# Hand-over from routing to experts: rows from slots by transposes, held gate loads, a shorter first row load

## What is computed

```
def hier_moe(h, w_group, b_group, w_expert, b_expert, w_gate, w_up, w_down):
    xf = xt.astype(F32)
    g_logits = xf @ w_group + b_group
    g_prob = jax.nn.softmax(g_logits, axis=-1)
    g_idx = jnp.argmax(g_logits, axis=-1)
    e_logits = (xf @ w_expert + b_expert).reshape(-1, N_GROUPS, EXP_PER_GROUP)
    e_sel = jnp.take_along_axis(e_logits, g_idx[:, None, None], axis=1)[:, 0]
    top_v, top_i = lax.top_k(jax.nn.softmax(e_sel, axis=-1), TOP_K)
    ...
    for e in range(N_EXPERTS):
        he = jax.nn.silu(xt @ w_gate[e]) * (xt @ w_up[e])
        y = y + combine[:, e:e + 1] * (he @ w_down[e]).astype(F32)

xp = gated_merge(xp, ...)                       # x += mixing part (through w_out)
xp = xp + hier_moe(rmsnorm(xp, g_ffn[l]), ...)  # x += experts
```

## Time and profile before

| | us |
|---|---|
| median of 3 runs | 1005.37 |
| lowest, highest | 1004.75, 1006.37 |
| profiled execution, its own time | 1005.73 |
| its span, first to last instruction | 1003.9 |
| the rest of its time, around the span | 1.8 |

### The profile page before, as it was taken

The page is one execution under the profiler, slowest core; times in us unless marked ns, Lnnn a source line. Parts: engine busy times, 40 slices in busy tenths (PEclk is TensorE's granted clock), DMA queues, the critical chain, the costliest instruction groups (busy, mean ns, idle before and its releaser), DMA issues.

```text
span 1003.9 us, 12085 instructions
## 1 busy us (share of the span) xinstructions
PE 986.0 (98%) x4614; PEld 810.5 (81%) x4614; DVE 674.6 (67%) x983; ACT 522.4 (52%) x700; POOL 150.5 (15%) x184
## 2 busy tenths in 40 slices
PE   9999999999999999999999999999999999999995
PEld 6888888888887887877877888789788888888884
DVE  6486875346656653443448457686889889888883
ACT  6744322345545553332452304544588687887783
POOL 1010001121120311121130000012012112121111
PEclk9999999999999999999999999999999999999999
DMA  9476567874361655973284345137899999999994
GB/s 348 144 221 145 134 142 234 252 224 159 135 232 61 244 195 188 348 283 140 95 314 164 105 173 224 55 128 286 345 401 403 380 404 391 392 405 380 403 404 93
DMA packets 125987, 245.27 MB, mean 244 GB/s; under 512 B 69072, under 2 KB 69376, under 8 KB 113600
## 3 DMA queue, kind: packets, MB, share of 16 engines
q1 hardware_dynamic: 105520, 172.51, 47.2%
q0 software_dynamic: 20112, 71.37, 21.6%
q10 hardware_dynamic: 288, 0.52, 0.2%
HBM read 203.07 MB, written 52.08 MB: 254 GB/s over the span
## 4 chain that ended last, share of the span: by engine, by line
PE 67%; issue 26%; DVE 3%; POOL 3%; ACT 1%; DMA 0%; POOLq 0%; SPq 0%; ACTq 0%; DVEq 0%
PE ps L481 16%; PE ps L483 16%; PE ps L482 16%; PE ps L1874 3%; PE ps L1875 3%; PE ps L1847 2%; PE ps L1909 2%; POOL x_exp L858 1%; POOL out_y L869 1%; PE ps L2017 1%; PE ps L2033 1%; PE ps L1968 1%; DVE w_lo L453 1%; PE ps L1891 1%; PE ps L2024 1%
## 5 line engine op out<-in xcount | busy, mean ns | idle before, releaser
L481 PE MATMUL ps<-w_hi,s_hi 128*128 128x512 f32 x640 | 255.6, 399 | 0.8 <-issue 0.8
L483 PE MATMUL ps<-w_lo,s_hi 128*128 128x512 f32 x640 | 249.7, 390 | 0.0
L482 PE MATMUL ps<-w_hi,s_lo 128*128 128x512 f32 x640 | 249.3, 390 | 0.0
L481 PEld LDWEIGHTS ps<-w_hi,s_hi 128*128 128x128 f32 x640 | 120.3, 188 | 26.4 <-issue 2.2
L482 PEld LDWEIGHTS ps<-w_hi,s_lo 128*128 128x128 f32 x640 | 120.3, 188 | 25.3 <-issue 1.0
L483 PEld LDWEIGHTS ps<-w_lo,s_hi 128*128 128x128 f32 x640 | 120.1, 188 | 25.4
L417 DVE TENSOR_TENSOR w_lo<-raw,w_hi 128x2048 fp32r<-128x2048 f32 x40 | 91.6, 2290 | 47.4 <-ACT w_hi L412 47.2
L1016 ACT ACTIVATE stage<-ps,x_rstd 128x512 f32<-128x512 f32 x64 | 44.0, 688 | 140.4 <-PE ps L483 140.0
L412 ACT CAST w_hi<-raw 128x2048 fp32r<-128x2048 f32 x40 | 76.2, 1910 | 16.8 <-DMA raw<-in_w_in 11.2
L453 DVE TENSOR_TENSOR lo_x<-raw_x,hi_x 128x2048 fp32r<-128x2048 f32 x32 | 72.5, 2286 | 6.9 <-ACT hi_x L430 6.9
L453 DVE TENSOR_TENSOR lo_x<-raw_x,w_hi 128x2048 fp32r<-128x2048 f32 x32 | 72.6, 2287 | 5.3 <-ACT w_hi L430 5.2
(11 more groups left out here) (308 smaller groups left out, 1830.7 us busy)
## 6 DMA issues: line engine op xcount, KB each, us to landing
raw<-in_w_in SPq DMA_DIRECT2D x30, 1024.0 KB, 8.5
raw_x<-in_w_gate SPq DMA_DIRECT2D x30, 1024.0 KB, 24.3
raw_x<-in_w_down SPq DMA_DIRECT2D x18, 1024.0 KB, 23.7
raw_x<-in_w_up SPq DMA_DIRECT2D x16, 1024.0 KB, 21.2
raw<-in_w_up SPq DMA_DIRECT2D x16, 1024.0 KB, 22.3
raw<-in_w_down SPq DMA_DIRECT2D x14, 1024.0 KB, 23.2
x_slots<-in_c_empty SPq DMA_DIRECT2D x4, 2112.0 KB, 21.1
x_exp<-x_slots POOLq DMA_DIRECT2D x16, 528.0 KB, 13.6
```

The lines of the kernel that those rows point to most:

```text
L481: nc.tensor.matmul(out, s_h, w_h, start=first, stop=False)
L482: nc.tensor.matmul(out, s_l, w_h, start=False, stop=False)
L483: return nc.tensor.matmul(out, s_h, w_l, start=False, stop=last)
```

## The change

There are six parts, all in the hand-over:

1. `BY_PRODUCT` goes from 3 to 2: `rows_a` is loaded after the dispatches of three tiles, not two, and only the last two tiles are placed by a one-hot product. DVE makes two one-hot matrices.
2. `slot_rows` uses transposes in place of float32 matmuls with the identity, and stands first in its PSUM banks.
3. PE's order changes, and two groups of transposes of the identity into otherwise unused banks are added (`keep_busy`, 12 and 6).
4. DVE scales the last tile's rows after `choose` and not ahead of it, in two halves: the first ahead of `place_first`, the second behind it (with a new semaphore `last_row`, for which PE waits).
5. ACT takes a root of a constant into a spare word right after the exponentials of the fourth tile, so that the table load for Sqrt stands there.
6. SP issues m = 6 and m = 7 only when all ten dispatches have landed, and `x_exp[0]` is loaded with its notes alone (128 rows x 32 floats).

```diff
--- before.py
+++ after.py
@@ -59,7 +59,7 @@
 LAM_INIT = 0.8 - 0.6 * math.exp(0.0)
 SINK = ROWS
 FILL_AT = 26
-BY_PRODUCT = 3
+BY_PRODUCT = 2
 FIRST_PARTS = ((0, 1), (1, 2), (2, 4), (4, 6), (6, 8))
 
 
@@ -156,7 +156,8 @@
     end[0] = GSUB + 4 * (DV + 2 * DK)
     r_bias = after("r_bias", [P, NG + NE], f32)
     gffn_col = after("gffn_col", [P, KC], f32)
-    lam = after("lam", [P, 4], f32)
+    lam_spare = after("lam", [P, 8], f32)
+    lam, spare = lam_spare[:, 0:4], lam_spare[:, 4:5]
     eps = after("eps", [P, 1], f32)
     x2_rms = after("x2_rms", [P, 2, TT], f32)
     x_rstd = after("x_rstd", [P, TT], f32)
@@ -344,7 +345,7 @@
     sel_ready, pos_ready, npass_ready = sem("sel_ready"), sem("pos_ready"), sem("npass_ready")
     row_ready, dispatched, meta_ready = sem("row_ready"), sem("dispatched"), sem("meta_ready")
     x_loaded = [sem("x_loaded0"), sem("x_loaded1")]
-    slots_ready, onehot_ready = sem("slots_ready"), sem("onehot_ready")
+    slots_ready, onehot_ready, last_row = sem("slots_ready"), sem("onehot_ready"), sem("last_row")
     sample_kept, rows_a_in = sem("sample_kept"), sem("rows_a_in")
     x_tr, xhi_ready, xlo_ready = sem("x_tr"), sem("xhi_ready"), sem("xlo_ready")
     silu_ready, act_ready = sem("silu_ready"), sem("act_ready")
@@ -612,6 +613,8 @@
                     sp.wait_ge(blocks_used, LAST - 2)
                 elif m < SPL:
                     sp.wait_ge(blocks_used, LAST - 1 + m - WR)
+                    if m >= SPL - 2:
+                        sp.wait_ge(dispatched, 16 * 2 * TT)
                 elif m == SPL:
                     sp.wait_ge(y_init, 16 * TT)
                     sp.wait_ge(sample_kept, 16)
@@ -854,7 +857,9 @@
 
         def load_rows(j, i):
 
-            if j == 0:
+            if j == 0 and i == 0:
+                dma(x_exp[0][:, D_MODEL:XW], x_slots[CAP * EXPERT[0]:CAP * EXPERT[0] + P, D_MODEL:XW]).then_inc(x_loaded[0], 16)
+            elif j == 0:
                 dma(x_exp[i % 2][:, :], x_slots[CAP * EXPERT[i]:CAP * EXPERT[i] + P, :]).then_inc(x_loaded[i % 2], 16)
             else:
                 pool.indirect_dma_start(out=x_exp[i % 2][:, :], out_offset=None, in_=x_slots,
@@ -1201,6 +1206,7 @@
                 source_hi(4, t, (0,))
             if n:
                 exps(ORDER[n - 1])
+        own(nc.scalar.activation(spare, eps[:, :], ACT.Sqrt))
         source_hi(4, ORDER[PT], (1,))
         square_x2(ORDER[PT])
         root_x2(ORDER[PT])
@@ -1633,10 +1639,10 @@
                     source_lo(2, PT)
 
 
-        def rows_of_tile(t):
+        def rows_of_tile(t, c0=0, c1=D_MODEL):
             rows = slice(0, P if t < PT else SAMPLE)
-            v.scalar_tensor_tensor(rows_out[rows, t, 0:D_MODEL], x2[rows, t, :], x2_rms[rows, 1, t:t + 1],
-                                   gffn[rows, :], ALU.mult, ALU.mult)
+            return v.scalar_tensor_tensor(rows_out[rows, t, c0:c1], x2[rows, t, c0:c1], x2_rms[rows, 1, t:t + 1],
+                                          gffn[rows, c0:c1], ALU.mult, ALU.mult)
 
         def root_of_tile(t):
             rows = slice(0, P if t < PT else SAMPLE)
@@ -1727,9 +1733,10 @@
         source_lo(4, ORDER[PT], (1,))
         place_rows(ORDER[PT - 1])
         root_of_tile(ORDER[PT])
-        rows_of_tile(ORDER[PT])
         choose(ORDER[PT])
+        rows_of_tile(ORDER[PT], 0, COLS)
         place_first(ORDER[PT])
+        rows_of_tile(ORDER[PT], COLS).then_inc(last_row, 1)
         place_rows(ORDER[PT])
 
         def count_slots():
@@ -2116,29 +2123,37 @@
         def placed_rows(n, half):
             t = ORDER[TT - BY_PRODUCT + n]
             pe.wait_ge(onehot_ready, n + 1)
+            if n == BY_PRODUCT - 1 and half:
+                pe.wait_ge(last_row, 1)
             for k in range(4):
                 last = mm(ps[:, half, k * P:(k + 1) * P], rows_out[:, t, rows_of(half, k)], onehot[:, n, :],
-                          start=n == 0 and k == 0, stop=n == BY_PRODUCT - 1 and k == 3)
+                          start=False, stop=n == BY_PRODUCT - 1 and k == 3)
             return last
 
         def slot_rows(half):
             pe.wait_ge(rows_a_in, 16)
             for k in range(4):
-                mm(ps[:, half, k * P:(k + 1) * P], rows_a[:, rows_of(half, k)], ident, start=False, stop=False)
+                mm(ps[:, half, k * P:(k + 1) * P], rows_a[:, rows_of(half, k)], ident, start=k == 0, stop=False,
+                   is_transpose=True)
+
+        def keep_busy(bank, count):
+            for _ in range(count):
+                transpose(ps[:, bank, 0:P], ident, ident)
 
         positions(PT - 1)
         logits(ORDER[PT], (0,))
         pe.wait_ge(p_evacuated, x2_done(ORDER[PT]))
         source(4, ORDER[PT], x2[:, ORDER[PT], :], (1,))
-        placed_rows(0, 0)
+        keep_busy(1, 12)
         logits(ORDER[PT], (1,))
-        placed_rows(0, 1)
-        for half in range(2):
-            placed_rows(1, half)
-        positions(PT)
         for half in range(2):
             slot_rows(half)
-            placed_rows(2, half).then_inc(x_tr, 1)
+            placed_rows(0, half)
+        positions(PT)
+        pe.wait_ge(x2_squared, TT)
+        keep_busy(3, 6)
+        for half in range(2):
+            placed_rows(1, half).then_inc(x_tr, 1)
         pe.wait_ge(row_ready, TT)
         for s in range(TT):
             last = mm(ps[:, 7, TT * NE:(TT + 1) * NE], ones16[:, :], sel[:, s, :], start=s == 0, stop=s == TT - 1)
```

## The result

The changed kernel took 1008.35 us in the median of 20 runs (1005.85 to 1011.85). The kernel before took 1006.31 beside it, also of 20 (1004.75 to 1009.69). The ratio is 1.0018, with a 95% interval of 1.001 to 1.0027: slower by 0.2%, or 1.8 us, where I forecast 1.2 us faster. The median lies above my range, and 4.15 us above the 1004.2 that I forecast. Of these, 0.94 us is the kernel before, whose three runs shown ahead had a median of 1005.37; the other 3.2 is the forecast: the medians are 2.04 apart, where I had 1.2 the other way.

What follows compares the result with a forecast made beforehand. The backlogged DMA weight stream was taken to set the end, with PE close behind. Starting the stream 1.2 us earlier gave 1005.37 - 1.2 = 1004.2 us, range 1002.6 to 1006.8.

Steps and rivals of the forecast that it cites:

- The bound: Kernel end: the last w_down landing sets it; an earlier stream brings it forward by up to 1.62 us; chance 0.45.
- PE sets the end: Rival, kernel end: the end follows PE, gaining 1.9 to 3.3 us, middle 2.6, giving 1002.8; chance 0.25.
- The hand-over on DVE and PE: Last tile: onehot at 694.7, dest at 697.1, expert 0 at about 698.0, 5.1 us earlier than before.
- eight products are left, 1.9: PE behind the last onehot: only eight one-hot products remain, taking 1.9 us, to 696.9.
- The dispatch: Last dispatch: issued by 700.0, lands undisturbed in 2.63 us, at 702.6, where before it took 5.6.
- the landing of the row tile: x_exp[1] on POOL's queue: with a third of the engines from the start it takes 3.9 us, to 708.5.
- the row tile is late behind the gates: Rival, hand-over: x_exp[1] lands at 711.2 to 713.4, delaying m = 8; middle 2.1 us later, 1007.5; chance 0.15.
- the landing at about 707 that the rule gave: Row tile in the hand-over: queues taking turns give it half the engines from the start, landing at about 707.
- The gain that I counted on: Weight stream behind the hand-over: m = 8's bytes could move from 710.4, not 711.6, gaining 1.2 us.
- the 0.5 MB saved on `x_exp[0]`: Hand-over loads: the notes-only load saves 1.3 us of bytes, already included in the stream's sum.
- The loads' landing: Held gates: m = 7 lands at 710.6, its split ends at 712.5, expert 1 begins at about 714.2.
- The clock: Rival, expert 0: starting at 1.2 GHz costs PE 2.8 to 5.6 us; 1005.4; chance 0.15, including gain otherwise lost.

Runs made afterwards that it cites:

- after: The changed kernel with all six parts, against the kernel before: 1008.35 us, ratio 1.0018.
- before_hold: The kernel before with only the hold added (m = 6 and 7 wait for all dispatches): 1009.51 us, ratio 1.0031 to the kernel before.
- late_rows: Changed kernel without holding m = 6 and 7; PE transposes expert 1's row tile behind expert 0's fourth block, not ahead: ratio 1.0004 to the kernel before.
- after_early8: Changed kernel, hold kept; m = 8 and m = 10 no longer wait for the row tiles of experts 1 and 0: ratio 0.9997 to the kernel before.
- late_rows_m8_now: late_rows with m = 8 and m = 10 waiting for the dispatches alone, so m = 8 goes out with the row tile: ratio 1.0013 to the kernel before.
- after_nokeep: The changed kernel without the two keep_busy calls (12 and 6 identity transposes): ratio 1.0004 to the kernel before.
- before: The kernel ahead of the change, the reference of all ratios: 1006.31 us beside the changed kernel.
- before_notes: The kernel before with only the notes-only load of x_exp[0], 0.5 MB fewer: ratio 0.9996 to the kernel before.
- late_rows_m8_notes: late_rows with POOL loading x_exp[0]'s notes ahead of the row tile and m = 8 waiting for the notes alone: ratio 0.9993 to the kernel before.
- late_rows_m8_ninth: late_rows_m8_notes with m = 8 released by the ninth of ten dispatches, m = 9 by the notes: 1005.18 us, ratio 0.9982 to the kernel before.

## Why the prediction was wrong

**The bound: right.** I said that the end follows the landing of the last `w_down` block and with it the start of the stream, not PE. ACT's wait of 1.19 us stands in after, before_hold shows a late stream costing time with PE on time, and late_rows an early PE gaining nothing. My "PE sets the end" rival is out for this change, but it isn't far off: after_early8 and late_rows_m8_now end by PE.

**The hand-over on DVE and PE: right, with one term wrong by a factor of two.** `onehot` was forecast at 694.70, which is H+9.85, and came at H+9.85. `dest` was forecast at H+12.25 and came at H+12.28. DVE's wait of 0.31 for the table is gone. Expert 0 was forecast at H+13.15 and came at H+14.16. The error is in "eight products are left, 1.9": I took each row of the count in the earlier trace rows for one product, but the call issues four to a half and eight rows are recorded for them, so two rows of 0.25 make a product. Eight products are the `x16` of 4.00 us at 697.35, 2.1 more than I had. That expert 0 was only 1.0 late is luck: I had also put 1.1 us for `x_hi` and `x_lo` behind the products, and in the trace expert 0's first block begins right behind them, on parts made from the first half. It did no harm, as 4.00 us of waiting follow.

**The dispatch: right.** 2.86 us for a forecast of 2.63, seen by POOL at H+18.0; I had H+17.75.

**The step that failed is the landing of the row tile: "0.54 MB at 0.137 take 3.9, to 708.5 if it gets that third from the start. I take this value."** In after it landed 8.6 us behind its issue, where I had 5.9. The third is right, the start isn't. The DMA queues of after in 707 to 709 and in 709 to 711 (packets, MB, share of 16 engines; q1 is SP's, q0 POOL's):

```profile
q1 hardware_dynamic: 101, 0.81, 96.4%
q0 software_dynamic: 2, 0.01, 1.0%
...
q1 hardware_dynamic: 77, 0.52, 63.7%
q0 software_dynamic: 67, 0.28, 35.2%
```

SP's queue has had the engines to itself since 706; POOL's begins at about 709 and then gets its 35%. 0.54 MB at 0.14 a us from there is 3.9 us, which is 713; it landed at 713.8. So this is the rival that I had called "the row tile is late behind the gates", with its own number: "At 8.6 it lands at 711.2 and m = 8 is issued 1.0 later than before". In the trace m = 8 is 1.4 us later, and the changed kernel 1.8 us. I gave it 0.15, although the only rows of that load beside SP's, had 8.6 as their least; I discounted them because a backlog stood ahead of them. They were the nearest rows and I should have taken them. The rival's price was nearly right, 2.1 us later against the 1.8 measured; that closeness is part luck, as 2.1 was the middle of two landings. What was wrong was the chance.

The Trainium skill (DMA: Bandwidth & Descriptors, Queues, rings and completion order) lets a DMA engine take turns between its queues. From 709 on the 77 and 67 packets look like turns; they aren't of one size (0.52 MB and 0.28 MB), so POOL's queue has a third of the engines and not the half that I worked out from that rule. In 707 to 709 the 2 packets against 101 don't look like turns, and the landing at about 707 that the rule gave for this load was not seen in any kernel in which SP issued at the same time. The tile took 8.6, 8.7, 9.0, 9.1 and 8.6 us in after, before_hold, after_early8, late_rows_m8_now and after_nokeep.

**The gain that I counted on: "the stream begins at 704.0 ... m = 8's bytes could move from 710.4 on".** It hangs on that same landing. Before, the engines move m = 6 and 7 while PE and DVE work out the last dispatch; they are free at that time. Held, these 2.1 MB are moved when everything else wants to move: the dispatch is home at H+18.0 and not at H+21.5, 3.4 us earlier, and the 5.1 us that 2.1 MB take at 0.41 are put behind it. I had this in the sum as bytes, and set against it a pause that I took to be there before and gone after. It is not gone. The DMA share in 712 to 716 is 0.48 and 0.44, since m = 8 waits for the same tile in both kernels, and the tile comes late. The balance as such held: in after_early8, where m = 8 doesn't wait for the tile, the stream moved 0.59 MB more than before's in the 200 us, which at 0.41 MB a us is 1.4 us, where I had 1.2. But there PE still stood for the tile and set the end, so the late landing spoils the gain in both ways. One term of the sum was wrong without harm: the 0.5 MB saved on `x_exp[0]` are moved in a pause, as before_notes shows, and gain nothing.

**The loads' landing: m = 7 was forecast at H+25.75** and came at 714.0, H+26.9, so expert 1 could not have begun on the forecast even without the tile; ACT stands 4.26 and 2.26 us for the two gates.

**The clock.** It was 1.00 through the hand-over where before had 0.50 at 692, so my condition for that rival didn't come. It did fall to 0.50 from about 712.2 to 719.1, first while PE stood for the tile and then in the work behind, and so the fourth block took 4.5 us, from 715.51 to 720.00, where I had 2.8 for a block. These 1.7 us are about as much as the 1.5 us by which expert 1 is late. As the stream sets the end, they aren't in the result. The Trainium skill (TensorE: Matmul & The Clock Gate, Part 4: PE-mode transpose) says of PE-mode transposes that they don't count as PE-busy for the clock in the same way. The windows of after_nokeep and after above don't agree with that: with the identity transposes 1.00 (693 to 695, H+5.8 to H+7.8), without them 0.50 in the same part of the program (690 to 692, H+5.9 to H+7.9). In after_nokeep PE stood idle for 1.46 us until 687.21, just before the clock fell; in after the 12 transposes fill that time.

## What to carry to other kernels

When two engines are full, ask the landing times, not the busy shares, which of them has slack: only what moves the start or the bytes of the backlogged stream moves the end, and only until the other engine's slack (here 1.8 us) is used up. Don't clear the way for an urgent small transfer by holding large ones that fill an idle time; shorten the pause of the stream instead, here by releasing one large load one landing earlier and holding the next until the notes have landed, which gave POOL's row tile a start of 3 us on it. Where a load shares the engines with another that starts at the same moment, price it by rows in which it did so, even if something else was different in them.

## What the hardware showed that I had not expected

- POOL's queue lags when SP's loads begin with it. The 528 KB row tile took 8.6 to 9.1 us in the five kernels in which SP issued megabyte loads within 0.4 us of it, and 3.8 to 3.9 alone. With SP's next load 1.5 us behind, it took 3.9 (late_rows_m8_notes). It took 4.1 in late_rows_m8_ninth, where a single load of SP's was 2 us ahead and the next came 3 us behind. What makes the lag wasn't tried further.
- An indirect dispatch lands in 2.8 to 3.0 us into empty engines, and in 5.6 to 6.8 behind two gate blocks. That doesn't matter in itself, as those blocks have to be moved anyway.
- With eighteen float32 transposes of the identity the granted clock stayed at 1.00 through the hand-over; without them it was 0.50 from 688 to 694 and from 698 to 701 (after against after_nokeep). With them the last dispatch was issued 1.0 us earlier, at H+12.96 and not H+13.99. A difference in the whole time can't be told.
- In the last block, too, the clock fell to 0.50 in four of the thirteen profiled executions, and that block took 7.02 in late_rows_m8_ninth against 5.45 in before, where the clock stayed at 1.00.
